# A two-layer decoder trunk on one core: small inputs on another DMA queue, the first two chunks of the output projections interleaved, and a few VectorE steps moved

## The chip, the core and the metric

The kernel runs on one core of one Trainium2 chip. The core has a matrix engine (TensorE, PE in the profile; its weight loads are PEld), a vector engine (VectorE, DVE), a scalar engine (ScalarE, ACT), a general engine (GpSimd, POOL) and a queue engine (SyncE, SP). The engines run side by side, each through its own list of instructions, and wait for one another by semaphores. Transfers between HBM and the on-chip memory (SBUF) are issued by an engine's queue and carried out by 16 DMA engines. Matmul results stand in PSUM banks of 128 rows by 512 f32 values. The metric is the device time of one execution in microseconds (us); less is better.

## What is computed

The reference, cut to what matters (sequence 256, width 2048, one self-decoder layer A and one cross-decoder layer B, MLP width 8192):

```
c_act = silu(c)
for layer in (0, 1):
    if layer == 1: k_sh, v_sh = shared_kv(x, c_act, kv_ada_w, ...)   # modulated norm, then w_k, w_v
    mod = c_act @ ada_w[layer] + ada_b[layer]
    shift_t, scale_t, gate_t, shift_m, scale_m, gate_m = split(mod, 6)
    h = rms_norm(x, g) * (1 + scale_t) + shift_t
    y = mixer_a(h) if layer == 0 else mixer_b(h, k_sh, v_sh)         # each ends in "@ w_o"
    x = x + gate_t * y
    h = rms_norm(x, g2) * (1 + scale_m) + shift_m
    x = x + gate_m * (square(relu(h @ w1)) @ w2)
```

mixer_a has three groups of dilated window attention over 8 heads of 128, mixer_b differential attention over 8 heads of 256; queries and keys are RMS-normed and rotated (which needs sine and cosine of the positions).

## The kernel before

**Weights.** All weights are read once, as one stream of 800 pieces of 256 x 512 values (512 KB). A piece lands in one of 6 slots of `w_raw`; ACT rounds it to `w_hi` (line 848), DVE subtracts to get the rest, `w_lo` (line 1221), and PE multiplies: per piece 2 tiles of 128 rows of K x 2 tiles of 128 tokens x 3 products (hi·hi, lo·hi, hi·lo) = 12 matmuls of 128 x 512 into the two banks of `main[0]` or `main[1]`. A chunk is 512 output columns: 8 pieces (4 in layer A's output projection). Consecutive chunks use `main[0]` and `main[1]` in turn. SP issues piece n when PE has finished piece n - 6. DVE runs some pieces ahead of PE.

**Modulation.** `ada` is a stream of pieces of 1 MB. For the first two sections (the start) they land in four places (`ada_raw`, `qT`), and PE (line 660) and DVE (lines 1248, 1252) share the product with `c_act`; PE's line 669 adds DVE's part, ACT turns the sum into the scale and shift of the next 256 columns, and only then can `hT` be made for them. Eight such rounds run through the start, each with three weight pieces. All later `ada` pieces are one DVE instruction each of 128 x 2048 (line 1235, 2.35 us), put after chosen weight pieces by hand-written lists (`ADA_Q` for the sections computed during layer B's queries and the first key/value chunks). When 16 pieces are summed, PE transposes or adds the sum over partitions.

**Order.** Each engine's program is written out by hand: `chunk(pieces, side)` runs the weight step of each piece and, at a numbered place between pieces, the steps in `side`. A DVE step `update(c, back)` waits until PE has finished all but the last `back` of the pieces that DVE has split, then multiplies the chunk's two banks by the gate, frees them (`read_out`), and adds to x.

**Start.** SP issues the vectors (`vecs`), x (2 MB), the positions, the bias columns (80 KB), the lambda vectors (256 KB) and then the stream of `ada` and weight pieces. DVE waits for all three small inputs (`small_in`), computes `bias0`, the lambda products and the angles, and only then takes up its share of the first `ada` piece. ACT sums x's squares (line 955), takes the root (line 967), then exp, then sine and cosine, then its first weight piece. POOL waits for the sines (`trig_done`) and for the inverse root (`x_rstd`), then writes the normed x to `st_x` (line 1819), which PE transposes (line 468).

**Output projections.** `first_two` runs the first two chunks on PE together: both chunks over the first `early` pieces (2 of 4 in layer A, 6 of 8 in B), then chunk 0's remaining pieces, then chunk 1's. Between pieces stand the last attention steps, which produce the heads that the late pieces need: `head_transposes(j)` on PE, `heads[j]` on ACT (line 1013), `lows[j]` on DVE (line 1436). `gemm_leave` and `gemm_arrive` form the passage from the last chunk of one stage to the first of the next: the two token tiles are finished one after the other, and DVE's `arrive` holds the order of its steps there. With `keep` (into layer B) each normed unit is also copied to `work` (line 1457), which frees the transposes' bank.

Of the kernel before, what the change touches and what calls it, by code (L numbers as in the profile page):

```python
# [16 lines left out]

# [8 lines left out]
P = 128  # L26
# [4 lines left out]
NC = 512  # L31
PK = 2
PIECES = KT // PK
# [50 lines left out]
def after(*lists, first=0):  # L84

    return [(c, j) for c, js in enumerate(lists, first) for j in js]
# [17 lines left out]
ADA_Q = after((), (0, 5, 7), (0, 5, 7), (0, 5, 7), (0, 3, 6), (0, 5, 7), (0,))  # L104
# [4 lines left out]
def trunk(nc, x_in, vecs_in, pos_in, gain_rot_in, gain_cols_in, subg_in, lamb_in, ada_in, bias_cols_in, bias_rows_in, w_in, out):  # L109
    ctx = ExitStack()  # L110
    with ctx:
# [148 lines left out]
        def _(sp):  # L260
# [30 lines left out]
            sp.dma_start(xs[:, :, :], x_in.rearrange("(t p) d -> p t d", p=P)).then_inc(x_in_done, 16)  # L291
            sp.dma_start(pos_i[:, :], pos_in).then_inc(small_in, 16)
            sp.dma_start(modc[:, :, :], bias_cols_in).then_inc(small_in, 16)
            sp.dma_start(st_a[:, 0:NC], lamb_in.partition_broadcast(P)).then_inc(small_in, 16)
# [62 lines left out]
        def _(pe):  # L357
# [274 lines left out]
            def first_two(pairs, early, side):  # L632

                order = [(c, j) for js in (range(early), range(early, pairs)) for c in range(2) for j in js]
                for i, (c, j) in enumerate(order):
                    if j == 0:
                        claim_main(c)
                    s = next_piece()
                    if c == 0:
                        pe.wait_ge(tr_free[j % 2], head_claim[j] + 1)  # L640
                    piece(c, pairs, hT_hi, hT_lo, j, s, range(T)).then_inc(mm_done, 1)
                    for step in side.get(i, ()):
                        step()
# [196 lines left out]
        def _(act):  # L840
# [253 lines left out]

            act.wait_ge(eps_set, 1)
# [113 lines left out]
        def _(dve):  # L1209
# [336 lines left out]
            def arrive(sections, g, keep=False, soon=False):  # L1546
# [13 lines left out]
                if soon:  # L1560
                    early = [modulation, leave(0), sum_part, tile_recip(0), stage_unit(0)]
                side = {0: early if soon else [],
                        2: [*([] if soon else early), units[0], leave(1, 2), *kept[0]],
                        3: [units[1], tile_recip(1), stage_unit(2), *kept[1], counted],
# [138 lines left out]
            dve.wait_ge(consts, 3)  # L1703
            dve.wait_ge(gain_in, 16 * 3)
# [7 lines left out]
            def all_exps():  # L1712
# [5 lines left out]
                                   2: [merge(1, 1, False), merged, lows[2], all_rows[3]], 4: [lows[3], all_rows[2]]})  # L1718
            chunk(2, PIECES // 2, {1: [lambda: ada_piece(0)], 2: [update(0)], 3: [lambda: ada_piece(1)], 4: [update(1)]})
# [77 lines left out]
            section_chunk(10, {2: [update(0)], 4: [update(1)]})  # L1797
# [7 lines left out]
        def _(pool):  # L1805
# [51 lines left out]
            pool.wait_ge(trig_done, 1)  # L1857
# [101 lines left out]
```

## Time and profile before

| | us |
|---|---|
| median of 3 runs (lowest, highest) | 2451.81 (2448.53, 2453.15) |
| the profiled execution, its own time | 2452.71 |
| its span, first to last instruction | 2450.9 |
| PE busy | 2397.9 |
| DVE busy | 1801.0 |
| ACT busy | 1244.9 |
| POOL busy | 52.0 |

The profile gives each instruction's start and length, the idle time of its engine before it and what released it, the granted clock of TensorE and the busy share of the DMA engines. Times of places are us from the span's start. A busy PE isn't PE at its peak: matmuls overlap, so one of 128 x 512 is shown with 0.39 us while the next starts 0.23 us after it.

### The profile page before, as it was taken

How to read it: one execution, taken by the hardware profiler on the slowest of the kernel's cores; microseconds unless marked ns; L12 is line 12 of the kernel's file. 1: busy time of each engine (PE TensorE's matmuls, PEld its weight loads, DVE VectorE, ACT ScalarE, POOL GpSimd, SP SyncE). 2: the span in 40 equal slices, each digit the busy share in tenths (PEclk: the TensorE clock that was granted, in tenths of full speed). 3: DMA queues.
4: the chain of work that ended last, by engine and by line, in shares of the span. 5: the costliest groups of instructions: out<-in, count | busy, mean ns of one | idle time of the engine just before them, and what ended most of it. 6: DMA issues, size and time to landing. Idle time of an engine off the chain costs nothing.

```text
span 2450.9 us, 28446 instructions
## 1 busy us (share of the span) xinstructions
PE 2397.9 (98%) x11121; PEld 1985.9 (81%) x11121; DVE 1801.0 (73%) x2150; ACT 1244.9 (51%) x2078; POOL 52.0 (2%) x82
## 2 busy tenths in 40 slices
PE   6999999999999999999999999999999999999999
PEld 5887888877888888888887878878788888888887
DVE  8968887878888778778697887767786455455554
ACT  4375565566444444534446575664653443443442
POOL 2100000001000000000001000000100000000000
PEclk9999999999999999999999999999999999999999
DMA  9978877956989888888795876656795555555555
GB/s 388 415 273 290 324 286 275 351 199 244 359 340 340 317 305 325 308 306 331 285 355 203 335 278 241 240 207 232 281 360 183 189 184 194 190 188 191 188 189 172
DMA packets 150485, 665.27 MB, mean 271 GB/s; under 512 B 16880, under 2 KB 17360, under 8 KB 120912
## 3 DMA queue, kind: packets, MB, share of 16 engines
q1 hardware_dynamic: 150352, 663.46, 74.2%
q8 instruction: 88, 1.44, 0.2%
q14 instruction: 45, 0.37, 0.0%
HBM read 661.30 MB, written 2.10 MB: 271 GB/s over the span
## 4 chain that ended last, share of the span: by engine, by line
PE 80%; DVE 8%; ACT 7%; DMA 3%; issue 2%; SPq 0%; POOL 0%; ACTq 0%; DVEq 0%; POOLq 0%
PE main L385 22%; PE main L383 22%; PE main L384 22%; DVE w_lo L1221 3%; DVE acc L1235 2%; ACT w_hi L848 2%; PE main L397 2%; PE main L399 2%; PE main L398 2%; PE tr L468 2%; DMA w_raw<-w 1%; ACT st_a L888 1%; PE tr L660 1%; ACT st_b L874 1%; PE tr L510 1%
## 5 line engine op out<-in xcount | busy, mean ns | idle before, releaser
L848 ACT ACTIVATE w_hi<-w_raw 128x1024 fp32r<-128x1024 f32 x800 | 842.6, 1059 | 962.8 <-DMA w_raw<-w 959.6
L1221 DVE TENSOR_TENSOR w_lo<-w_raw,w_hi 128x1024 fp32r<-128x1024 f32 x800 | 968.9, 1222 | 421.5 <-ACT w_hi L848 418.0
L383 PE MATMUL main<-w_hi,hT_hi 128*128 128x512 f32 x1840 | 732.8, 398 | 0.1
L385 PE MATMUL main<-w_hi,hT_lo 128*128 128x512 f32 x1840 | 718.4, 390 | 0.0
L384 PE MATMUL main<-w_lo,hT_hi 128*128 128x512 f32 x1840 | 716.4, 389 | 0.0
L1235 DVE SCALAR_TENSOR_TENSOR acc<-ada_raw,c_act,acc 128x2048 f32<-128x2048 f32 x165 | 387.4, 2348 | 36.6 <-DMA ada_raw<-ada 35.4
L385 PEld LDWEIGHTS main<-w_hi,hT_lo 128*128 128x128 f32 x1840 | 345.6, 188 | 73.6
L384 PEld LDWEIGHTS main<-w_lo,hT_hi 128*128 128x128 f32 x1840 | 346.3, 188 | 71.0 <-issue 1.2
L383 PEld LDWEIGHTS main<-w_hi,hT_hi 128*128 128x128 f32 x1840 | 346.1, 188 | 70.8 <-issue 1.4
L383 PE MATMUL main<-w_hi,mid_hi 128*128 128x512 f32 x960 | 375.5, 391 | 0.0
L385 PE MATMUL main<-w_hi,mid_lo 128*128 128x512 f32 x960 | 373.8, 389 | 0.0
L384 PE MATMUL main<-w_lo,mid_hi 128*128 128x512 f32 x960 | 373.4, 389 | 0.0
L384 PEld LDWEIGHTS main<-w_lo,mid_hi 128*128 128x128 f32 x960 | 180.3, 188 | 37.6 <-issue 0.5
L385 PEld LDWEIGHTS main<-w_hi,mid_lo 128*128 128x128 f32 x960 | 180.2, 188 | 37.6
L383 PEld LDWEIGHTS main<-w_hi,mid_hi 128*128 128x128 f32 x960 | 180.2, 188 | 37.3 <-issue 0.5
L397 PE MATMUL main<-w_hi,hT_hi 128*128 128x512 f32 x240 | 98.0, 408 | 8.3 <-DVE hT_lo L1525 4.4
L399 PE MATMUL main<-w_hi,hT_lo 128*128 128x512 f32 x240 | 94.3, 393 | 0.0
L398 PE MATMUL main<-w_lo,hT_hi 128*128 128x512 f32 x240 | 94.0, 392 | 0.0
L397 PEld LDWEIGHTS main<-w_hi,hT_hi 128*128 128x128 f32 x240 | 45.4, 189 | 20.6 <-DVE w_lo L1221 7.2
L399 PEld LDWEIGHTS main<-w_hi,hT_lo 128*128 128x128 f32 x240 | 45.3, 189 | 9.9
L398 PEld LDWEIGHTS main<-w_lo,hT_hi 128*128 128x128 f32 x240 | 45.5, 190 | 8.2
L1734 DVE TENSOR_TENSOR mid_lo<-tr,mid_hi 128x512 fp32r<-128x512 f32 x64 | 41.1, 683 | 12.5 <-ACT mid_hi L1166 12.5
(236 smaller groups left out, 1749.1 us busy)
## 6 DMA issues: line engine op xcount, KB each, us to landing
w_raw<-w SPq DMA_DIRECT2D x800, 512.0 KB, 4.1
ada_raw<-ada SPq DMA_DIRECT2D x208, 1024.0 KB, 6.9
qT<-ada SPq DMA_DIRECT2D x16, 1024.0 KB, 9.9
gate<-bias_rows SPq DMA_DIRECT2D x4, 1024.0 KB, 6.3
xs<-x SPq DMA_DIRECT2D x1, 2048.0 KB, 8.1
out<-xs SPq DMA_DIRECT2D x3, 512.0 KB, 5.8
out<-xs SPq DMA_DIRECT2D x2, 256.0 KB, 2.5
st_a<-lamb SPq DMA_DIRECT2D x1, 256.0 KB, 9.2
```

The costliest lines, as they stand in the source:

```text
L383: pe.matmul(acc_ps[:, :], hi[:, kt, tc], w_hi[:, s, wc], start=(kt == 0), stop=False)
L384: pe.matmul(acc_ps[:, :], hi[:, kt, tc], w_lo[:, s, wc], start=False, stop=False)
L385: last = pe.matmul(acc_ps[:, :], lo[:, kt, tc], w_hi[:, s, wc], start=False, stop=(kt == PK * pairs - 1))
L397: pe.matmul(acc_ps[:, :], hi[:, kt, tc], w_hi[:, s, wc], start=(kt == 0), stop=False)
L398: pe.matmul(acc_ps[:, :], hi[:, kt, tc], w_lo[:, s, wc], start=False, stop=False)
L399: last = pe.matmul(acc_ps[:, :], lo[:, kt, tc], w_hi[:, s, wc], start=False, stop=(kt == PK * pairs - 1))
L468: last = pe.transpose(tr[b][:, at:at + P], source(k, t), ident[:, :])
L510: last = pe.transpose(tr[b][:, k * P:(k + 1) * P], rows[:, quarter, k * P:(k + 1) * P], ident[:, :])
L848: act.activation(w_hi[:, s, :], w_raw[:, s, :], ACT.Copy).then_inc(hi_done, 1)
L1221: dve.tensor_tensor(w_lo[:, s, :], w_raw[:, s, :], w_hi[:, s, :].bitcast(F32), ALU.subtract).then_inc(lo_done, 1)
L1235: ins = dve.scalar_tensor_tensor(out=total[:, :], in0=piece, scalar=c_act[:, kt:kt + 1], in1=total[:, :], op0=ALU.mult, op1=ALU.add)
L1734: dve.tensor_tensor(mid_lo[:, kt:kt + PK, :], tr[kp][:, :].rearrange("p (k n) -> p k n", k=PK), mid_hi[:, kt:kt + PK, :].bitcast(F32), ALU ...
```

## The change

Six edits:

1. x, the positions, the bias columns and the lambda vectors are issued by ACT's queue, as ACT's first four instructions, no more by SP's. SP goes from `vecs` straight to the `ada` and weight pieces.
2. POOL no longer waits for the sines before it stages x; DVE waits for them instead, after the start, ahead of the first attention group.
3. In `first_two` the pieces after `early` alternate: chunk 0's, chunk 1's, chunk 0's, chunk 1's. The host lays the weights out in that order. `update(0)` behind it waits for one piece more (back 3, was 4), in both layers.
4. In layer A's projection DVE makes `lows[2]` ahead of the last merge of the attention (`merge(1, 1)`, `merged`), no longer behind it.
5. In `arrive` the copy of the first unit (`kept[0]`) stands behind `units[1]`, one place later.
6. `ADA_Q`: one modulation piece goes from behind piece 6 of the first key/value chunk to behind piece 3 of the third, where it is the 16th and last of its section.

The number of instructions stays the same; only the engine that issues four of the DMAs differs.

```diff
-ADA_Q = after((), (0, 5, 7), (0, 5, 7), (0, 5, 7), (0, 3, 6), (0, 5, 7), (0,))
+ADA_Q = after((), (0, 5, 7), (0, 5, 7), (0, 5, 7), (0, 3), (0, 5, 7), (0, 3))
...
             sp.dma_start(cols_in[0:96, :], vecs_in).then_inc(vec_in, 16)
-            sp.dma_start(xs[:, :, :], x_in.rearrange("(t p) d -> p t d", p=P)).then_inc(x_in_done, 16)
-            sp.dma_start(pos_i[:, :], pos_in).then_inc(small_in, 16)
-            sp.dma_start(modc[:, :, :], bias_cols_in).then_inc(small_in, 16)
-            sp.dma_start(st_a[:, 0:NC], lamb_in.partition_broadcast(P)).then_inc(small_in, 16)
...
-                order = [(c, j) for js in (range(early), range(early, pairs)) for c in range(2) for j in js]
+                order = [*itertools.product(range(2), range(early)), *((c, j) for j in range(early, pairs) for c in range(2))]
...
+            act.dma_start(xs[:, :, :], x_in.rearrange("(t p) d -> p t d", p=P)).then_inc(x_in_done, 16)
+            act.dma_start(pos_i[:, :], pos_in).then_inc(small_in, 16)
+            act.dma_start(modc[:, :, :], bias_cols_in).then_inc(small_in, 16)
+            act.dma_start(st_a[:, 0:NC], lamb_in.partition_broadcast(P)).then_inc(small_in, 16)
             act.wait_ge(eps_set, 1)
...
-                        2: [*([] if soon else early), units[0], leave(1, 2), *kept[0]],
-                        3: [units[1], tile_recip(1), stage_unit(2), *kept[1], counted],
+                        2: [*([] if soon else early), units[0], leave(1, 2)],
+                        3: [units[1], *kept[0], tile_recip(1), stage_unit(2), *kept[1], counted],
...
             dve.wait_ge(consts, 3)
+            dve.wait_ge(trig_done, 1)
...
-                                   2: [merge(1, 1, False), merged, lows[2], all_rows[3]], 4: [lows[3], all_rows[2]]})
-            chunk(2, PIECES // 2, {1: [lambda: ada_piece(0)], 2: [update(0)], 3: [lambda: ada_piece(1)], 4: [update(1)]})
+                                   2: [lows[2], merge(1, 1, False), merged, all_rows[3]], 4: [lows[3], all_rows[2]]})
+            chunk(2, PIECES // 2, {1: [lambda: ada_piece(0)], 2: [update(0, 3)], 3: [lambda: ada_piece(1)], 4: [update(1)]})
...
-            section_chunk(10, {2: [update(0)], 4: [update(1)]})
+            section_chunk(10, {2: [update(0, 3)], 4: [update(1)]})
...
             pool.wait_ge(vec_full, 1)
-            pool.wait_ge(trig_done, 1)
             pool.wait_ge(x_rstd, 1)
```

Three places in the engines' programs. First the start, SP's queue before:

```order
L290 DMA sm<-vecs 96x128
L291 DMA xs<-x 128x2x2048
L292 DMA pos_i<-pos 128x2
L293 DMA modc<-bias_cols 128x160
L294 DMA st_a<-lamb 128x512
L301 DMA ada_raw<-ada 128x2048 x2
L301 DMA qT<-ada 128x2048
```

and ACT's program in the changed kernel:

```order
L1092 DMA xs<-x 128x2x2048
L1093 DMA pos_i<-pos 128x2
L1094 DMA modc<-bias_cols 128x160
L1095 DMA st_a<-lamb 128x512
L1098 ACT_TABLE_LOAD
L1098 ACTIVATE c_act<-vec 128x16
```

Four DMAs left SP's queue, where they stood ahead of the first `ada` piece, and stand now ahead of all of ACT's work.

Second, DVE in layer A's output projection (`work` is the merge of the heads, `hT_lo<-tr0` is `lows[2]`, `gate<-tr1` a row of the MLP's gate), before:

```order
L1221 TENSOR_TENSOR w_lo<-w_raw,w_hi 128x1024
L1397 SCALAR_TENSOR_TENSOR work<-work,corr8,ov 128x128 x4
L1311 MEMSET scratch 128x1
L1436 TENSOR_TENSOR hT_lo<-tr0,hT_hi 128x512
L1303 TENSOR_TENSOR gate<-tr1,gate 128x512
```

and now:

```order
L1222 TENSOR_TENSOR w_lo<-w_raw,w_hi 128x1024
L1437 TENSOR_TENSOR hT_lo<-tr0,hT_hi 128x512
L1398 SCALAR_TENSOR_TENSOR work<-work,corr8,ov 128x128 x4
L1312 MEMSET scratch 128x1
L1304 TENSOR_TENSOR gate<-tr1,gate 128x512
```

The low part went ahead of the merge. Third, DVE in the passage into layer B (`work<-tr0` is the copy, the `hT_lo` behind it `units[1]`), before:

```order
L1543 TENSOR_TENSOR xs<-xs,st_a 128x512
L1457 COPY work<-tr0 128x4x128
L1221 TENSOR_TENSOR w_lo<-w_raw,w_hi 128x1024
L1525 TENSOR_TENSOR hT_lo<-st_b,hT_hi 128x2x128 x2
L1501 RECIPROCAL rstdx<-rmsx 128x1
```

and now:

```order
L1544 TENSOR_TENSOR xs<-xs,st_a 128x512
L1222 TENSOR_TENSOR w_lo<-w_raw,w_hi 128x1024
L1526 TENSOR_TENSOR hT_lo<-st_b,hT_hi 128x2x128 x2
L1458 COPY work<-tr0 128x4x128
L1502 RECIPROCAL rstdx<-rmsx 128x1
```

The copy went behind the low parts and stands now ahead of the reciprocal.

## Rows read from the trace of the kernel before

**Rows 1.** The page, part 1: busy us, share of span, instructions.

```profile
PE 2397.9 (98%) x11121; PEld 1985.9 (81%) x11121; DVE 1801.0 (73%) x2150; ACT 1244.9 (51%) x2078; POOL 52.0 (2%) x82
```

**Rows 2.** Timeline of SP, start: start us, length us, engine, line, operation.

```profile
1.19 0.42 SPq L291 DMA_DIRECT2D xs<-x  x1
...
2.65 0.81 SPq L294 DMA_DIRECT2D st_a<-lamb  x1
3.50 1.01 SPq L301 DMA_DIRECT2D ada_raw<-ada  x2
```

**Rows 3.** DMA issues: KB, median us from issue to landing.

```profile
xs<-x SPq DMA_DIRECT2D x1, 2048.0 KB, 8.1
```

**Rows 4.** Timeline of PE, start; in brackets idle before and releaser.

```profile
14.45 1.84 PE L660 MATMUL tr<-c_act,ada_raw 128*128 128x1 f32 x8 [11.51 <-DMA ada_raw<-ada]
16.83 1.86 PE L660 MATMUL tr<-c_act,ada_raw 128*128 128x1 f32 x8 [0.54 <-DMA ada_raw<-ada]
22.90 1.09 PE L468 MATMUL tr<-ident,st_x 128*128 128x128 f32 x4 [4.20 <-POOL st_x L1819]
...
27.05 1.84 PE L669 MATMUL tr<-ones,acc 128*128 128x1 f32 x8
```

**Rows 5.** Timeline of DVE, start.

```profile
11.90 0.17 DVE L1621 COPY bias<-modc 128x16 f32<-128x16 f32 x1 [3.85 <-DMA st_a<-lamb]
...
19.35 0.16 DVE L1572 RECIPROCAL rstdx<-rmsx 128x2 f32<-128x2 f32 x1
...
23.81 2.73 DVE L1252 SCALAR_TENSOR_TENSOR acc<-qT,c_act,acc 128x512 f32<-128x512 f32 x3
```

**Rows 6.** Timeline of POOL, start.

```profile
21.79 6.15 POOL L1819 TENSOR_SCALAR st_x<-xs,rstdx 128x256 f32<-128x256 f32 x6 [12.31 <-ACT cos L1111]
```

**Rows 7.** The chain that ended last, 60 to 128 us: PE's addition, round by round.

```profile
69.46 0.89 PE tr L669 x8
...
82.64 0.89 PE tr L669 x8
...
109.55 1.05 PE tr L669 x8
...
124.41 0.91 PE tr L669 x8
```

**Rows 8.** Windows: stretch, length, busy of engines, PEclk, DMA share, GB/s.

```profile
1320.00:1323.50 3.50, 3.50 (x12) 2.78 (x12) 2.23 (x4) 0.84 (x2) 1.15 (x2) 0.51 0.00 0
...
111.50:115.20 3.70, 3.70 (x13) 2.98 (x11) 3.46 (x7) 1.75 (x4) 0.00 (x0) 0.54 0.99 412
```

**Rows 9.** Timeline of PE, layer A's output projection.

```profile
544.50 0.47 PE L397 MATMUL main<-w_hi,hT_hi 128*128 128x512 f32 x1 [1.31 <-DVE hT_lo L1436]
...
549.42 0.47 PE L397 MATMUL main<-w_hi,hT_hi 128*128 128x512 f32 x1 [0.64 <-DVE hT_lo L1436]
...
552.27 0.39 PE L397 MATMUL main<-w_hi,hT_hi 128*128 128x512 f32 x1
```

**Rows 10.** Timeline of DVE, from that projection to its end.

```profile
553.40 1.29 DVE L1584 TENSOR_TENSOR st_b<-main,gate 128x512 f32<-128x512 f32 x2
...
578.06 0.49 DVE L1511 TENSOR_SCALAR st_x<-xs,rstdx 128x512 f32<-128x512 f32 x1
```

**Rows 11.** Timeline of DVE, the passage into layer B.

```profile
1317.45 0.68 DVE L1457 COPY work<-tr 128x512 f32<-128x512 f32 x1
```

**Rows 12.** Timeline of PE, the passage into layer B.

```profile
1319.75 0.50 PE L397 MATMUL main<-w_hi,hT_hi 128*128 128x512 f32 x1 [1.83 <-DVE hT_lo L1525]
...
1322.18 1.05 PE L416 MATMUL tr<-ident,st_x 128*128 128x128 f32 x4
```

**Rows 13.** Timeline of DVE, third key/value chunk.

```profile
1467.68 0.28 DVE L1350 CUSTOM_DVE_ANT_0 sm<-sc,masks 128x128 f32<-128x128 f32 x1 [2.18 <-issue]
```

**Rows 14.** Timeline of PE, third key/value chunk.

```profile
1470.87 1.88 PE L522 MATMUL tr<-acc,ones 128*128 128x512 f32 x4
```

**Rows 15.** Timeline of DVE, layer B's output projection.

```profile
1673.78 1.29 DVE L1584 TENSOR_TENSOR st_b<-main,gate 128x512 f32<-128x512 f32 x2
```

More of the change, by code:

```diff
@@ L18 @@
+import itertools
 import math
@@ L1915, in first_two @@
         w = rows.reshape(4, -1, P, PK * NC)
-        two = [w[c, js] for js in (slice(0, early), slice(early, None)) for c in range(2)]
-        return np.concatenate([*two, *w[2:4]]).reshape(-1, PK * NC)
+        late = w[0:2, early:].swapaxes(0, 1).reshape(-1, P, PK * NC)
+        return np.concatenate([w[0, :early], w[1, :early], late, *w[2:4]]).reshape(-1, PK * NC)
     qkv = f["a_w_qkv"][0].reshape(D, GROUPS, 3, 2, NC)
```

## The prediction

> **What bounds the kernel now.** I read the page first, then PE's waits, then the timelines around every place that the change touches. PE is busy for 98% of the span [rows 1]; what can be gained is 53 us in which it idles, and stretches in which its clock is low. The idle time is in few places: the start, where PE waits 11.51 us for the first `ada` piece and 4.20 us for the first normed x [rows 4], the two output projections with the passages behind them, and the start of layer B. All six edits aim at such places. So the question for each is which wait ends last there, and what is late next.
>
> Sums are made against the profiled execution, 2452.7 us (span 2450.9 and 1.8 around it). The median of the runs shown is 0.9 lower, so 0.9 comes off at the end.
>
> **Edit 1, the four DMAs on ACT's queue.** What it removes: SP issues x at 1.19 and its first `ada` piece at 3.50, behind four issues [rows 2]. Now that piece can go at about 1.19, 2.3 us earlier, and x at SP's old first place, about 0.46 earlier. The four issues cost ACT about 2.1 us (1.19 to the end of the fourth, 3.46) [rows 2], at nothing: ACT's next work needs the vectors, and its squares need x.
> What it adds: x and the small inputs now share the DMA engines with `ada` pieces, where they had them alone. Who waits for that? DVE can't do anything of the start before all three small inputs have landed; it wakes at 11.90, released by the last of them [rows 5]. Its chain from there to its last share of the first `ada` round ends at 23.81 + 2.73 = 26.54 [rows 5], and PE adds that share at 27.05 [rows 4]. From there PE runs round by round with hardly a gap. So each us by which the small inputs land later moves the whole start, and the early `ada` piece buys nothing, because DVE takes it up behind them.
> How late do they land? No row shows two queues at once. From below: they land with x's head start, 0.46 earlier. From above: every row of theirs takes turns with one row of an `ada` piece. Then x needs its 8.1 us [rows 3] about 1.6 times over, some +5, and the three small ones wait for three pieces of 1 MB, 3 x 2.38 = 7.1 (a piece lands each 16.83 - 14.45 = 2.38 us [rows 4]), together about +11. Between them: x goes first and whole, and two of the three small ones wait one `ada` piece each, 2 x 2.38 = +4.8, less 0.46: **+4.3**. I take this, since x is issued first and the trace's transfers went out in order of issue on the one queue.
> Carried through: DVE's share then ends at 26.54 + 4.3 = 30.8, PE adds at about 30.9, which is **+3.9** on 27.05.
> [...]
>
> **What of it comes back.** The rounds of the start are 82.64 - 69.46 = 13.18 us apart, as long as PE's own work. The last two pairs are longer: 109.55 - 82.64 = 26.91 for two rounds (+0.55), 124.41 - 109.55 = 14.86 (+1.68) [rows 7]. [...] With the stream 2.3 us earlier and the rounds 3.9 later the pieces are no longer late, and both excesses go: **-2.2**. Start in all: **+1.7**.
>
> **Edit 2, POOL without the sines.** POOL began at 21.79, released by ACT's cosine, while the root was inverted at 19.35 [rows 5, 6]. But behind PE's transposes stand 16 small matmuls and then the addition at 27.05, which also needs DVE's share (26.54). So at most 0.5 us, and nothing once DVE is late. **0**, down to -0.5. DVE's new wait for the sines passes at once: they are a hundred us old there.
>
> **Edits 3 and 4, layer A's projection.** PE stands 1.31 us at 544.50 for the low part of pair 2, and 0.64 at 549.42 for that of pair 3 [rows 9]; with the pipeline's refill these are 1.8 and 1.1 us. DVE idles over 2 us before the merge that stood ahead of the first, so the low part can be made there, and pair 3 is wanted one piece later, and a piece is 552.27 - 549.42 = 2.85 [rows 9]. Both gaps go on PE: -2.5 at the end of `first_two`.
> Does that last? DVE's timeline from its `update(0)` at 553.40 to the staging of the first unit at 578.06 [rows 10] has no idle time but 0.64 us for ACT: weights, three modulation pieces, three updates. PE's unit(0) waits for that staging. So behind 553.40 DVE is the pacer, and PE's gain counts only as far as `update(0)` begins earlier. It now waits for chunk 0's last piece, which stands one later. PE would end it at about 542.9 (544.50 less the gap) + three pieces of 2.75 + the transposes and sums between, 1.3 = 552.4, so `update(0)` starts at about 552.6: **-0.8** instead of -2.5. The rest becomes a longer wait of PE at unit(0). Behind the waiting `update(0)` on DVE stand the weights of the next chunk, two pieces ahead of PE: hidden. The bank must be free before PE's next chunk at about 555.2; 552.6 + 1.3 = 553.9 leaves 1.3 us.
>
> **Edit 3 in layer B.** No low part is waited for there in the late pieces, so the order gains nothing. `update(0)` began at 1673.78 without waiting [rows 15]; it now waits for one piece more, some 1.6 us, and frees its bank about 1.3 us before PE wants it. DVE has slack behind that. **0**; if the cover fails, up to +1.4.
>
> **Edit 5, the copy.** PE waits 1.83 us until 1319.75 for the low part of `units[1]` [rows 12]; the copy of 0.68 us [rows 11] stood in its way on DVE: **-0.7**. The copy now delays the staging of the next unit by 0.15 us, hidden by the 6 matmuls between. Right behind the gap the clock falls: 0.51 from 1320.00 to 1323.50 [rows 8]. The 6 matmuls take 1322.18 - 1319.75 = 2.43 us [rows 12], against 1.4 for half a piece. PE's gap of 1.31 us at 544.50 had no such fall behind it, and the new gap is about as long. So I take the fall as gone: 1.0 there and 0.5 in the transposes, **-1.5** (0 if it stays).
>
> **Edit 6, the modulation piece.** Taken from a place where DVE had work but PE didn't wait: 0. Put where DVE idles 2.18 us before 1467.68 [rows 13]. It takes 2.35 us, so the mask step comes some 0.6 us later; PE asks for the finished sum at 1470.87 [rows 14], about 2.4 us after it. **0**, up to +1 if the transfer lands late.
>
> **Sum.** 2452.7 + 1.7 - 0.8 - 0.7 - 1.5 = 2451.4; less 0.9: **2450.5**. No change that can be told: a measurement of this kernel tells about 0.2%, 4.9 us, that is below 2446.9 or above 2456.7.
>
> **Rivals.**
> [...] 0.2.
> *Row by row in turn.* Small inputs at +11, start +10.6 - 2.2 = +8.4: 2452.7 - 0.9 + 8.4 - 3.0 = 2457.2, slower. It decides from +10 on; the place is DVE's wake-up (11.90 before). 0.15.
> *PE's gain in layer A lasts*, if DVE has slack that I don't see: 1.7 less than the forecast, 2448.8. Against it stand 25 us of DVE without a gap. 0.1.
> *The clock still falls* behind the shorter gap, or at another place: 1.5 to 3 more, 2452 to 2453.5. 0.1.
> The forecast itself: 0.45.
>
> **Range and chances.** The range reaches over the forecast, both small rivals and most of the two outer ones: 2445.5 to 2457.5. Faster by over 0.2%: most of the first rival, 0.2. Slower: most of the second, with something for a wait that I cost at nothing, 0.14. Within: 0.66.
>
> **What would show it.** DVE's wake-up (11.90 before) between 15 and 17, PE's first addition near 31, and additions 13.2 us apart to the end of the start, with no low clock near 112. In layer A both waits for the low parts gone, and a wait of some 2 us or more before the first unit near 578. A gap of 1.1 to 1.3 before `units[1]` is multiplied, at full clock behind it. No wait of PE at the sum in the third key/value chunk. The forecast is wrong if DVE wakes before 12 or after 20, or if DVE isn't the pacer up to the unit at 578.

## The result: slower, by what DVE waits for at the start

The changed kernel takes 2454.15 us in the median of 21 runs (2451.74 to 2460.88), the kernel before 2449.9 us in the median of 21 (2446.73 to 2453.15). The ratio is 1.0021, with a 95% interval from 1.0016 to 1.0027: slower by 3.9 to 6.6 us, where I had forecast no change (2450.5, and 1.3 us below the runs shown). 2454.15 lies inside my range of 2445.5 to 2457.5, but that is owed to the width of the range: DVE's wake-up, on which the forecast rests, came 3.1 us later than I had it. The profiled execution of the changed kernel is the median one, 2454.15 us, with a span of 2452.4.

The start shows the loss at once. DVE, timeline of the changed kernel (columns as in [rows 5]):

```profile
19.32 0.17 DVE L1622 COPY bias<-modc 128x16 f32<-128x16 f32 x1 [11.26 <-DMA st_a<-lamb]
...
26.78 0.16 DVE L1573 RECIPROCAL rstdx<-rmsx 128x2 f32<-128x2 f32 x1
...
31.28 2.63 DVE L1253 SCALAR_TENSOR_TENSOR acc<-qT,c_act,acc 128x512 f32<-128x512 f32 x3
```

PE and POOL, the same stretch, answering to [rows 4] and [rows 6]:

```profile
11.29 1.84 PE L657 MATMUL tr<-c_act,ada_raw 128*128 128x1 f32 x8 [7.34 <-DMA ada_raw<-ada]
13.91 1.86 PE L657 MATMUL tr<-c_act,ada_raw 128*128 128x1 f32 x8 [0.78 <-DMA ada_raw<-ada]
29.10 1.09 PE L465 MATMUL tr<-ident,st_x 128*128 128x128 f32 x4 [13.32 <-POOL st_x L1821]
29.98 3.41 PE L657 MATMUL tr<-c_act,qT 128*128 128x1 f32 x16
33.97 1.86 PE L666 MATMUL tr<-ones,acc 128*128 128x1 f32 x8 [0.57 <-DVE acc L1253]
```

```profile
27.12 5.46 POOL L1821 TENSOR_SCALAR st_x<-xs,rstdx 128x256 f32<-128x256 f32 x6 [17.64 <-DVE rstdx L1573]
```

The first `ada` piece is 3.2 us earlier (11.29 for 14.45) and buys nothing. DVE wakes 7.4 us later (19.32 for 11.90), each step of its chain moves with it, and PE's first addition comes 6.9 us later (33.97 for 27.05). The wait that took the place of PE's 4.20 us is one of 13.32 us for the normed x.

Where the difference stands along the program: the start of the same matmul in two traces, subtracted, in us. The first column is its time in the trace of before that the prediction used. "Again" is a second profile of the kernel before (below).

| at (before) | place | changed, less before | changed, less before again |
|---|---|---|---|
| 27 | first addition | +6.9 | +7.7 |
| 128 | end of the start | +5.9 | +6.7 |
| 540 | ahead of A's low parts | +5.8 | +7.0 |
| 553 | end of `first_two` in A | +3.4 | +4.6 |
| 600 | A's projection done | +5.3 | +6.3 |
| 1290 | end of A's MLP | +5.2 | +6.3 |
| 1340 | passage done | +4.2 | +6.6 |
| 1434 | B's second chunk | +1.8 | +6.8 |
| 2440 | end | +1.5 | +6.4 |

Against the second profile the picture is plain: +6.7 at the start, -0.7 in layer A, and nearly level from there. Against the first one the loss melts away between 1290 and 1434. That is no merit of the change, as the second profile shows.

### The profile page after: what moved, and what is told of

It reads as the page before. It is cut to its first block, busy times and chain, and to the rows that moved or that the text cites. A ratio compares the mean times of both kernels' runs of the same rounds, so it can differ in the third digit from the quotient of the medians.

```text
span 2452.4 us, 28447 instructions
## 1 busy us (share of the span) xinstructions
PE 2393.1 (98%) x11121; PEld 1982.7 (81%) x11121; DVE 1801.3 (73%) x2150; ACT 1244.8 (51%) x2078; POOL 53.2 (2%) x82
## 4 chain that ended last, share of the span: by engine, by line
PE 81%; DVE 8%; ACT 6%; DMA 3%; issue 2%; ACTq 0%; SPq 0%; DVEq 0%
PE main L382 22%; PE main L380 22%; PE main L381 22%; DVE w_lo L1222 2%; ACT w_hi L845 2%; DVE acc L1236 2%; PE main L394 2%; PE main L396 2%; PE main L395 2%; DMA w_raw<-w 2%; PE tr L465 1%; ACT st_a L885 1%; PE tr L657 1%; ACT st_b L871 1%; DMA st_a<-lamb 1%
```

## The experiments

Every ratio is against the kernel before, run on the same chip in the same session, with its 95% interval. Where no ratio stands there was one profiled run. Different experiments ran on different chips, so two versions are compared with each other by their ratios.

**One part alone, and all but that part.** The first kernel is the one before with edit 1 (the four DMAs on ACT's queue) and nothing else.

```diff
-            sp.dma_start(xs[:, :, :], ...).then_inc(x_in_done, 16)
-            sp.dma_start(pos_i[:, :], pos_in).then_inc(small_in, 16)
...
+            act.dma_start(xs[:, :, :], ...).then_inc(x_in_done, 16)
+            act.dma_start(pos_i[:, :], pos_in).then_inc(small_in, 16)
...
             act.wait_ge(eps_set, 1)
```

> The kernel before with edit 1 alone: x and the three small inputs on ACT's queue; POOL still waits for the sines. Theory (the whole loss is the small inputs landing late): DVE wakes at 19 to 20 as in the changed kernel (19.32), PE's first addition comes at 34 to 35 (before 27.05, changed 33.97), about 2 us of that come back in the late rounds of the start, and the time is 4 to 6 us above the kernel before. Rival (the queue is not it; edits 3 to 6 lose it, or PE's clock falls more often for their sake): within 1.5 us of the kernel before.

Measured: 2458.74 us (5 runs), ratio 1.0039 (1.0027 to 1.0052). PE's first addition is at 34.24, POOL starts at 28.98 behind ACT's cosine. The theory holds for the start. The loss, 6.6 to 12.7 us by the interval, is larger than I expected and larger than that of the whole change; more on that below.

The second is the changed kernel with the four DMAs back on SP's queue, edits 2 to 6 kept.

> The changed kernel with edit 1 alone undone: the four DMAs back on SP's queue, edits 2 to 6 kept. Theory: DVE wakes at 11.9 and PE adds at 27.0 as before; layer A keeps its 0.65 us and the passage near 1320 its 0.3, so 0.5 to 2.5 us below the kernel before, and 5 to 7 below the changed kernel. Rival (edits 3 to 6 lose): 2 to 5 us above the kernel before.

Measured: 2448.48 us (11 runs), ratio 0.9999 (0.9990 to 1.0008). The first addition is at 26.69 again. So the changed kernel's loss comes from edit 1, and without edit 1 the other five together are worth nothing that can be told from zero. With edit 1 in place they give something back. At its end the trace of edit 1 alone lies 11.0 us behind the second profile of before, the changed kernel's 6.4. Of the difference, 0.6 us stand at the end of the start (edit 2, below), 1.0 more behind layer A's projection (0.7 of it edits 3 and 4) and 2.5 in a fall of the clock near 1434 that the changed kernel's trace doesn't have. How much of this stands in the medians is open.

**The order on ACT's queue.** The changed kernel, with the small inputs ahead of x.

```diff
-            act.dma_start(xs[:, :, :], ...).then_inc(x_in_done, 16)
             act.dma_start(pos_i[:, :], pos_in).then_inc(small_in, 16)
             act.dma_start(modc[:, :, :], bias_cols_in).then_inc(small_in, 16)
             act.dma_start(st_a[:, 0:NC], ...).then_inc(small_in, 16)
+            act.dma_start(xs[:, :, :], ...).then_inc(x_in_done, 16)
```

> The changed kernel with one thing altered: on ACT's queue the three small inputs are issued ahead of x, not behind it. Theory (place in ACT's queue decides: what is issued behind x shares the engines with the ada pieces and lands late): DVE wakes at 9 to 12 in place of 19.32, x lands a few us later (about 13 to 15), its sums and rstdx become the next late thing, and PE's first addition is at 26 to 29. The time is 5 to 8 us below the changed kernel. Rival (anything on ACT's queue is slow beside SP's stream, whatever its place): DVE wakes after 15 and the time is within 3 us of the changed kernel.

Measured: 2455.72 us (8 runs), ratio 1.0029 (1.0018 to 1.0039); not better than the changed kernel. DVE's first wait indeed ends near 11 (10.90), but now x lands at 19.4, 17.2 us after its issue (8.1 in [rows 3]), and the first addition is at 35.18. My estimate for x (13 to 15) was wrong. What stood behind other transfers on ACT's queue, beside SP's pieces, was late here, x too.

**Only x on ACT's queue**, the small inputs on SP's behind the vectors.

```diff
             sp.dma_start(cols_in[0:96, :], vecs_in).then_inc(vec_in, 16)
+            sp.dma_start(pos_i[:, :], pos_in).then_inc(small_in, 16)
+            sp.dma_start(modc[:, :, :], bias_cols_in).then_inc(small_in, 16)
+            sp.dma_start(st_a[:, 0:NC], ...).then_inc(small_in, 16)
...
             act.dma_start(xs[:, :, :], ...).then_inc(x_in_done, 16)
-            act.dma_start(pos_i[:, :], pos_in).then_inc(small_in, 16)
...
```

> The changed kernel with the three small inputs on SP's queue behind the vectors and ahead of the ada pieces; x alone stays on ACT's queue. Theory: the small inputs land at 8 to 10 and DVE has done its 3 us on them when the first ada piece lands (about 12 to 13); what is late next is x: if it lands by 12, PE's first addition is at 25 to 27, the time 1 to 5 us below the kernel before. Rival (x's transfer beside the stream is what costs): x lands after 15 and the first addition is later than 30.

Measured: 2446.9 us (11 runs), ratio 0.9989 (0.9980 to 0.9998), first addition at 25.03. It beats the changed kernel by about 0.3% (the two ratios), and the kernel before by 0.1%, just clear of its interval; the last version below, which also has x alone on ACT's queue, isn't clear of it.

**What a small transfer pays.** SP's first four `ada` pieces cut in two, then in four:

```diff
-                sp.dma_start(ada_start[s], av[i]).then_inc(ada_start_in[s], 16)
+                if i < len(ada_start):
+                    for h in range(2):
+                        sp.dma_start(ada_start[s][:, h * D // 2:(h + 1) * D // 2],
+                                     av[i][:, h * D // 2:(h + 1) * D // 2]).then_inc(...)
+                else:
+                    sp.dma_start(ada_start[s], av[i]).then_inc(ada_start_in[s], 16)
```

> The changed kernel with one thing altered: SP issues each of the first four ada pieces as two transfers of 512 KB in place of one of 1 MB (same bytes, same order). In the changed kernel the three small inputs land 2.8 us apart behind x (13.7, 16.5 and 19.2), against about 0.85 each when they are alone on one queue. Theory (a small transfer gets its turn on the DMA engines after one whole transfer of SP's, 2.4 us for 1 MB): they land about 1.6 apart, DVE wakes at 15 to 17, PE's first addition comes at 30 to 32, the time is 2 to 5 us below the changed kernel. Rival (the engines share by bytes or by time, or small transfers on ACT's queue are slow by themselves, whatever SP's transfers are cut into): still 2.8 apart, DVE wakes at 19 to 20, the same time.

> The changed kernel with SP's first four ada pieces issued as four transfers of 256 KB each. In halves the wake-up of DVE came at 16.04 instead of 19.32 (small inputs at 11.1, 12.8, 15.9). Theory (a turn costs as much as one of SP's transfers takes): the turn halves again, DVE wakes at 13 to 14.5, the first addition is at 28 to 29.5. Rival (a turn is a fixed number of descriptors or of bytes that halves already undercut): DVE wakes at 15.5 to 16.5 as with halves.

Measured: DVE wakes at 16.04 with halves and at 12.89 with quarters (19.32 whole), the first additions are at 30.70 and 27.54 (33.97). The medians are 2452.93 us (10 runs), ratio 1.0013 (1.0004 to 1.0022), and 2449.38 us (10 runs), ratio 1.0002 (0.9993 to 1.0011): cutting SP's rows takes back nearly the whole loss. That speaks against a share by bytes, for the bytes are the same in all three. The first two small inputs follow the size of the row: they land 2.7 and 2.9 us behind the transfer ahead whole (alone on SP's queue, in the two traces of before, the three take 2.5 and 2.4 us behind x in all: 9.34 to 11.80, 8.64 to 11.06), 1.3 and 1.6 in halves, 0.8 and 0.9 in quarters. The third doesn't in proportion (2.7, 3.1, 1.8), and the packets show why: in the changed kernel SP had come to its weight pieces by then, whose rows are of 4 KB (43 packets, 0.17 MB from 16 to 17 us). With halves, too, its rows beside the third were of 4 KB (68 packets, 0.28 MB from 12.5 to 13.5), and only with quarters of 2 KB (82 packets, 0.17 MB from 10.5 to 11.5).

Next, one small input alone behind x, the two others on SP's queue ahead of the pieces:

> The changed kernel with the first two small inputs on SP's queue ahead of the ada pieces, and only the third behind x on ACT's queue. Theory (each small transfer behind x costs one turn of 2.8 us): x lands at 9 to 10, DVE wakes 2.5 to 3 later, at 12 to 13.5, and the first addition comes at 27 to 29. Rival (sharing the engines costs a fixed 8 us, however many they are): DVE wakes after 16.

Measured: 2448.68 us (10 runs), ratio 0.9998 (0.9989 to 1.0007). A miss (I expected 12 to 13.5): DVE wakes at 10.76, released by the second small input, which was on SP's queue. The third landed at 10.1, for while SP's small rows were in flight ACT's queue took turns with small rows, not with 8 KB ones: from 8 to 9 us it had 54 packets and 0.10 MB, SP's 53 and 0.03. From 6 to 7, beside the positions' rows of 8 bytes, they had 51 each, 0.42 MB of it x. And x, which shared its turns with such rows only, landed at 8.6, no later than in the second profile of before.

A turn per transfer, or per row? The 1 KB of the positions cut in two transfers of 64 rows each, and then fetched twice, 128 rows more:

```diff
-            act.dma_start(pos_i[:, :], pos_in).then_inc(small_in, 16)
+            for h in range(2):
+                act.dma_start(pos_i[h * 64:(h + 1) * 64, :], pos_in[h * 64:(h + 1) * 64, :]).then_inc(...)
```

> The changed kernel with one thing altered: the 1 KB transfer of the positions on ACT's queue is issued as two of 512 B, so four small transfers stand behind x and not three; not one byte is added. Theory (each transfer behind x costs a turn of about 2.8 us while SP has its 1 MB pieces in flight, whatever its size): DVE wakes at 21.5 to 22.5 (19.32), the first addition comes at 36 to 37 (33.97), and the time is 2 to 3 us above the changed kernel. Rival (the cost goes by bytes or by descriptors): DVE wakes at 19 to 20 as before, same time.

```diff
+        pos_2 = sb("pos_2", [P, T], I32)
...
+            act.dma_start(pos_2[:, :], pos_in).then_inc(small_in, 16)
             act.dma_start(pos_i[:, :], pos_in).then_inc(small_in, 16)
```

> The changed kernel with one thing added: the 1 KB of positions (128 rows of 8 bytes) is fetched a second time, whole, into a tile of its own, ahead of the first, and DVE waits for that as well. Cut in two halves of 64 rows each, the positions cost nothing more (DVE woke at 18.95, changed kernel 19.32). Theory now (row for row: each row of a small transfer on ACT's queue waits for one row of SP's, 8 KB wide, so 128 rows cost what one ada piece takes, 2.4 to 2.8 us, and 64 cost half): DVE wakes at 21.5 to 22.3 and the first addition comes at 36 to 37, the time 2 to 3 us above the changed kernel. Rival (by bytes, or a lasting lag of ACT's queue as a whole that is there whatever stands in it): DVE wakes at 19 to 20.

Measured: cut in two, DVE wakes at 18.95, no later, with 2455.02 us (6 runs), ratio 1.0027 (1.0015 to 1.0038). My theory of a turn per transfer fell. Fetched twice, DVE wakes at 21.35, 2.0 us later, for 1 KB more. So the price goes by rows. The two queues in a window from 11 to 13 us of the changed kernel (packets, MB, share of 16 engines; q1 is SP's, q10 ACT's) and from 11 to 15 us of the kernel that fetches the positions twice show it directly:

```profile
q1 hardware_dynamic: 109, 0.79, 95.0%
q10 hardware_dynamic: 110, 0.02, 4.8%
```

```profile
q1 hardware_dynamic: 199, 1.50, 93.7%
q10 hardware_dynamic: 199, 0.00, 2.7%
```

109 to 110, and 199 to 199: one packet of ACT's queue for each of SP's, whether it holds 8 bytes or 8 KB. The equal counts agree with taking turns, and the two versions of the positions with turns of single rows, not of whole transfers. So do the counts in half microseconds of the changed kernel, 21 to 21 from 11.0 to 11.5 and 27 to 27 from 11.5 to 12.0: the small rows are spread among SP's and don't come in a burst. Turns of several rows these counts don't show.

But the kernel that fetches them twice took 2475.67 us (4 runs), ratio 1.0108 (1.0092 to 1.0125), and 2 us at the start don't make 21. The rest was spread over both MLPs, where PE never waited (busy for 90.00 us of 700 to 790 and for 500.00 of 1920 to 2420, at full clock) but was slower on the intermediates: from start to start 26 of their matmuls near 770 take 6.07 us (767.71 to 773.78, 233 ns each) in place of the changed kernel's 5.89 (767.84 to 773.73, 227 each). Over both MLPs nine in ten of them are 231 to 235 ns apart in place of 226 to 227, while those on `hT` stay at 227. My suspicion was the extra tile, since the tiles behind it, the MLPs' intermediates among them, had moved. So the spacer tile behind the small ones was shortened to make up for it:

```diff
-        sb("skip", [P, 112])
+        sb("skip", [P, 110])
```

> The kernel that fetches the positions twice, with the spacer behind the small tiles cut from 112 to 110 words, so that every tile behind it lies where it lies in the changed kernel. [...]
**A second look at the kernel before.**

> The kernel before, profiled a second time, to see which stretches of low clock are its own and which are one execution's. In the first trace it was low at 111.5 to 115.2, at 1320.0 to 1323.5 and at 1429.3 to 1432.7. Theory (they come and go from run to run; the first trace had more than usual, which is why it lay 2.8 us above the median): at least one of the three is missing here, the one at 1320 the likeliest, and the span is 1 to 3 us below 2450.9. Rival (they belong to the kernel, and edits 3 to 5 took them away): all three are there again.

Measured: 2447.74 us, a span of 2446.0, and none of the three stretches of low clock. The same window, 1415 to 1450 us (columns as in [rows 8]), of the kernel before in the first trace, before again, the changed kernel, and the kernel with x alone on ACT's queue:

```profile
1415.00:1450.00 35.00, 31.89 (x138) 26.10 (x137) 28.91 (x34) 30.12 (x81) 0.00 (x0) 0.95 0.72 264
```

```profile
1415.00:1450.00 35.00, 32.85 (x153) 27.11 (x152) 30.88 (x35) 29.87 (x80) 0.00 (x0) 1.00 0.79 298
```

```profile
1415.00:1450.00 35.00, 32.66 (x149) 26.86 (x148) 28.55 (x34) 33.31 (x86) 0.00 (x0) 1.00 0.70 263
```

```profile
1415.00:1450.00 35.00, 31.74 (x141) 26.02 (x141) 27.74 (x32) 29.26 (x79) 0.00 (x0) 0.95 0.68 247
```

A clock of 0.95 here is the fall near 1430, 3.4 us at 0.50 (1429.27 to 1432.69 in the first trace): 2.6 us between the two traces of before. It is there in eight of all seventeen traces (before, edit 1 alone, edits 2 to 6, x alone on ACT's queue, one small input behind x, the first two that fetch the positions twice, and the last version below), and absent in nine, the changed kernel and before again among them. The same kernel has it and has it not, so its absence from the changed kernel's trace is no merit of an edit. Ahead of it PE waits 2.58 to 3.46 us for the rotated queries; in the traces without it, at most 2.69. The falls near 112 and 1320 are in the first trace of before alone; one near 1297 is in one other trace, and one near 227 in those with halves and with quarters.

**Two more versions to beat both.** One has the small inputs on SP's queue behind the first `ada` piece, and DVE taking its share of that piece before it waits for them.

> A version to beat both: the changed kernel with x alone on ACT's queue, the small inputs on SP's queue behind the first ada piece, and DVE taking its share of that piece before it waits for the small inputs. Theory (DVE's chain of 12 us from the first ada piece to the addition sets the start): the first piece lands at 8 to 9, DVE goes on from there, and the first addition comes at 21 to 23 (25.03 with the small inputs ahead of the pieces, 27.05 before). The time is 2 to 4 us below that version and 3 to 6 below the kernel before. Rival (x becomes the late thing, as when it stood behind the small inputs and landed at 19): first addition after 25, no gain.

Measured: 2448.79 us (11 runs), ratio 0.9996 (0.9988 to 1.0005). The first addition is at 27.16. The first piece landed at 11.1 and not at 8 to 9, for it shared the engines with x (from 7 to 10 us SP's queue had 53.2% of them and ACT's 46.5%), and the second only at 16.9.

The other is the kernel with x alone on ACT's queue, edit 5 undone, and DVE's first low weights made behind its last share.

> A version to beat both: x alone on ACT's queue and the small inputs first on SP's, as in the version whose first addition came at 25.03; edit 5 undone (with it the two waits near 1320 are 1.71 + 1.17 us, without it 1.99 + 0.67); and in the first round DVE makes the low weights after its last share of the ada pieces, not ahead of it. Theory: DVE's chain from the first ada piece is 1.2 to 1.7 us shorter, first addition at 23.3 to 24, the waits near 1320 are 0.2 shorter in sum; 1.5 us below that version, 2.5 to 4 below the kernel before. Rival (the low weights, made later, are what PE's first main matmul then waits for, or the low clock of the start moves along): the first main matmul stays near 30.4 and nothing is gained.

Measured: 2447.42 us (11 runs), ratio 0.9999 (0.9990 to 1.0008). The first addition is at 24.69, only 0.3 earlier: with the weights out of the way DVE waits 1.43 us for the fourth `ada` piece. The first main matmul is at 30.73, and as in the version it was made from (30.43) the low clock of the start stands there: they come 0.43 us apart up to 34.7, and 0.23 behind that. Neither beats x alone on ACT's queue as far as these intervals tell.

## Why the prediction was wrong, step by step

**Edit 1, how late the small inputs land: the step that failed.** I took x to go "first and whole", 0.46 us earlier, and "two of the three small ones" to wait one `ada` piece each, 4.8 us; together +4.3 at the wake-up, where +7.4 came (19.32 for 11.90). The order of issue on one queue, my reason, is that of the landings before but for the positions: x at 9.34, they at 8.78, then 10.13, 11.80, and the first piece at 14.32. It said nothing of two queues. Both halves were too small. ACT's first square shows x: 11.00 in place of 9.36, so x is 1.6 later and not 0.46 earlier, 2.1 of the 3.1 us that I missed. From there to DVE's wake-up it is 8.3 us where it was 2.5, so 5.8 more and not 4.8: all three small inputs waited, landing 2.7 to 2.9 us behind x and each other. DMA issues of the changed kernel (KB, us from issue to landing):

```profile
xs<-x ACTq DMA_DIRECT2D x1, 2048.0 KB, 10.2
...
st_a<-lamb ACTq DMA_DIRECT2D x1, 256.0 KB, 17.0
modc<-bias_cols ACTq DMA_DIRECT2D x1, 80.0 KB, 14.8
...
pos_i<-pos ACTq DMA_DIRECT2D x1, 1.0 KB, 12.5
```

So they landed at 13.68, 16.56 and 19.22. The lower end, no delay at all, to which the first chance of 0.2 belongs, was further off than the forecast.

The 1 KB of the positions has as many rows as a piece of 1 MB, and each waits for a row of the piece. So the rule was my upper rival's, "row by row in turn", to which I had given 0.15. It took its price too high: a row's wait replaces its own time and isn't added to it (8.3 us in all for the three, where the rival had 2.5 + 7.1), and of x half had gone before the turns began. The two queues of the changed kernel from 2 to 5 us and from 7 to 10 us:

```profile
q10 hardware_dynamic: 116, 0.95, 85.6%
q1 hardware_dynamic: 61, 0.02, 3.3%
```

```profile
q1 hardware_dynamic: 90, 0.69, 54.2%
q10 hardware_dynamic: 85, 0.59, 46.6%
```

By 5 us ACT's queue had moved 0.95 MB of x, all but alone; from 7 on it had one packet in two (85 to 90). +7.4 at the wake-up lies about halfway between the forecast (+4.3) and the rival (+11, though its own terms, 5 + 7.1, make +12). No row of before shows x's head start, so from those rows the rule would have given too much; the middle value, in turn, had no rule behind it. These landings differ a little between executions: before again has the wake-up at 11.16, and the three other traces with the four DMAs and SP's rows as in the changed kernel (edit 1 alone, the positions cut in two, the spacer of 120 words) have it from 18.84 to 19.09. The shift is about 7 to 8 us in any pair.

**What comes back in the late rounds: 1.0, not 2.2.** The -2.2 took both excesses for the work of late `ada` pieces and of the low clock. Of lateness the first trace shows waits of DVE for `ada` pieces between 85 and 128, 0.8 us in all in `qT` and 0.3 in `ada_raw`; no run shows what either cause alone is worth. The low clock near 112 (in [rows 8]; 0.43 us from matmul to matmul in place of 0.23) is gone, but 6.9 first became 7.3 (82.64 in [rows 7] against 89.98) before 1.4 came back. And the fall near 112 is gone from the second profile of before as well, where the last round takes 13.9 us (109.53 to 123.46) in place of 14.7 (109.55 to 124.27): some of the 2.2 that I booked was that one execution's. Against the second profile 0.9 comes back. The chain of waits of the changed kernel, answering to [rows 7]:

```profile
89.98 0.89 PE tr L666 x8
103.16 0.89 PE tr L666 x8
130.31 0.89 PE tr L666 x8
```

The last two rounds take 27.15 us where PE's own work is 26.36, so not all of their excess went; the additions are not 13.2 us apart to the end, as I had said they would be. The start is +5.9 in place of +1.7, and that is the miss.

**Edit 2: worth 0.5 us, not 0.** From DVE's wake-up to PE's first addition it is 15.15 us in the kernel before (27.05 - 11.90) and with edit 1 alone (34.24 - 19.09), and 14.65 in the changed kernel (33.97 - 19.32) and with edits 2 to 6 alone (26.69 - 12.04). My reason, "nothing once DVE is late", was wrong: the sines hang on DVE's wake-up too, since DVE makes the angles, so POOL waited for them just as long when DVE was late. The sum doesn't suffer, because I had carried +4.3 at DVE on as +3.9 at PE and so booked 0.4 of it under edit 1.

**Edits 3 and 4, layer A: right in size and mechanism.** -2.45 at the end of `first_two` (forecast -2.5; the 0.47 that I added to each wait as a refill is the length at which the first matmul behind it is shown, and an estimate: in the trace of before it starts 0.30 us ahead of its next, 544.50 to 544.80, where the others are 0.23 apart), and behind the projection -0.5 against the first trace (forecast -0.8). Against the second it is -0.7, and also -0.7 in the kernel with edits 2 to 6 alone, and 0.0 with edit 1 alone. DVE is the pacer, and it took 1.9 us back. Only the place is another: not at the unit but one step ahead of it, at the low weights. DVE and PE of the changed kernel:

```profile
558.62 0.06 DVE L1312 MEMSET scratch<- 128x1 f32 x1 [0.98 <-PE main L396]
558.71 1.29 DVE L1585 TENSOR_TENSOR st_b<-main,gate 128x512 f32<-128x512 f32 x2
...
583.37 0.48 DVE L1512 TENSOR_SCALAR st_x<-xs,rstdx 128x512 f32<-128x512 f32 x1
```

```profile
577.70 0.50 PE L394 MATMUL main<-w_hi,hT_hi 128*128 128x512 f32 x1 [1.42 <-DVE w_lo L1222]
584.01 0.63 PE L413 MATMUL tr<-ident,st_x 128*128 128x128 f32 x4 [0.53 <-DVE st_x L1512]
```

From `update(0)` to the staging it is 24.66 us, as before (578.06 - 553.40 = 24.66 in [rows 10]). In layer B `update(0)` waits 1.79 us for PE (forecast 1.6), and no wait of PE follows: right.

**Edit 5, the copy: wrong in sign.** The wait got shorter by 0.28, and the copy, one place later, stood in front of the next unit, which cost 0.50. I had called that "0.15 us, hidden". PE at the two waits near 1320, first of the changed kernel, then of the kernel before again:

```profile
1324.44 0.47 PE L394 MATMUL main<-w_hi,hT_hi 128*128 128x512 f32 x1 [1.55 <-DVE hT_lo L1526]
1327.62 0.50 PE L394 MATMUL main<-w_hi,hT_hi 128*128 128x512 f32 x1 [1.01 <-DVE w_lo L1222]
```

```profile
1318.50 0.47 PE L397 MATMUL main<-w_hi,hT_hi 128*128 128x512 f32 x1 [1.83 <-DVE hT_lo L1525]
1321.07 0.50 PE L397 MATMUL main<-w_hi,hT_hi 128*128 128x512 f32 x1 [0.51 <-DVE w_lo L1221]
```

The last version above has edit 5 undone and 1.79 and 0.51; the one it was made from has 1.57 and 1.01. All thirteen traces with edit 5 have 1.55 to 1.57 and 1.01, and the three without it but the first 1.79 to 1.83 and 0.51. The first trace hid the second wait: in the low clock the 6 matmuls ahead of it, 0.43 us apart for 0.23, took 1 us longer, and DVE was done by then. So edit 5 is +0.2, not -0.7.

**The clock behind 1320: a chance taken for a property.** I booked -1.5 for a fall that [rows 8] show. It was absent in a second run of the same kernel, with the same wait of 1.83 us ahead of it. None of the other sixteen traces has one in the passage's place, so its cost was in that one execution and hardly in the median, and there was nothing to win. The falls at 1320 and 1429 account for 3.7 us between the two traces of before (1.1 and 2.6), more than the 2.8 by which the first lay above the median of 21; they are also why the changed kernel's trace seems to gain 3.4 us between 1290 and 1434.

**Edit 6: right.** DVE's piece starts at 1467.36 after 0.33 us of waiting for its transfer, the mask step behind it at 1469.64, and PE's sum at 1472.72 without a wait.

Together: the start +4.2 more than forecast, the clock +1.5, the copy +0.9, layer A +0.3, that is 6.9. Less 1.9, as the median of 21 runs of before is 2449.9 and not 2451.8, the forecast would have been 2450.5 + 5.0 = 2455.5, and 2454.15 was measured. The 1.3 us between them are not accounted for. The signs of five edits are small change beside one landing time.

## What to carry to other kernels

In these runs a small input with as many rows as a large one paid for standing on a second queue beside it (+7.4 us at DVE's wake-up, for three). So put it on the same queue, ahead, and give the second queue the one big transfer that nobody can start without (here 0.3% against the changed kernel, and 0.1% or nothing against the one before). A row in one trace that may be chance (a fall of the clock above all) is worth a second profile before it stands in a sum. And when a copy is moved past one waiting consumer, the next one in DVE's order is who pays (here 0.50 us, for 0.28 won).

## What was not expected of the hardware

Two queues took turns packet for packet, 109 to 110 while one moved 0.79 MB and the other 0.02, so what a small transfer paid went by its number of rows and by the size of the rows beside it.

Moving the MLPs' intermediates, and the tiles behind the spacer with them, by 32 bytes cost 18 to 19 us. In a window of MLP A, from 700 to 790 us, PE is busy throughout at full clock in both kernels, but it does 393 matmuls in place of 406: first the changed kernel, then the one with the spacer of 120 words.

```profile
700.00:790.00 90.00, 90.00 (x406) 74.67 (x406) 81.60 (x73) 35.07 (x33) 0.00 (x0) 1.00 0.93 353
```

```profile
700.00:790.00 90.00, 90.00 (x393) 72.89 (x392) 81.61 (x72) 35.06 (x33) 0.00 (x0) 1.00 0.91 344
```

Only the matmuls that read these tiles are slower, 233 ns from start to start in place of 227; those on `hT`, which had not moved, stay at 227. With the intermediates at 191136 all three kernels have 233, at 191104 the changed one and that with 104 words 227. Why an address should matter there isn't settled by these runs.
